# A hybrid decoder layer on one core: the indexer key centred and doubled by one product, rotary partners by VectorE shuffles, index scores in fours

## What is computed

```python
q_idx = partial_rope(q_idx.reshape(B, T, IDX_HEADS, IDX_DIM), positions)   # 8 heads x 64
k_idx = layernorm(k_idx, k_norm_w, k_norm_b)                               # one key of 64
k_idx = partial_rope(k_idx[:, :, None, :], positions)[:, :, 0, :]
w_idx = w_idx * (IDX_HEADS ** -0.5 * IDX_DIM ** -0.5)
...
s = jnp.einsum('bqhd,bsd->bqhs', qi, k_idx)
score = jnp.einsum('bqh,bqhs->bqs', wi, jax.nn.relu(s))
score = jnp.where(key_pos <= tq, score, -inf)
```

## Time and profile before

| | us |
|---|---|
| median of 3 executions | 726.9 (726.54 to 729.52) |
| the profiled execution, its own time | 728.42 |
| its span on the core | 726.7 |
| mean granted TensorE clock | 0.991 |
| PE busy | 705.7 |
| DVE busy | 434.0 |
| ACT busy | 296.2 |

### The profile page before, as it was taken

One profiled execution on the slowest core, in us unless ns is written; L12 is line 12 of the kernel. 1 busy time (PEld: TensorE's weight loads), 2 busy tenths in 40 slices (PEclk: granted clock), 3 DMA queues, 4 the chain that ended last, 5 costly groups with the idle time before them and its releaser, 6 DMA issues.

```text
span 726.7 us, 11020 instructions
## 1 busy us (share of the span) xinstructions
PE 705.7 (97%) x3962; PEld 552.7 (76%) x3962; DVE 434.0 (60%) x806; ACT 296.2 (41%) x472; POOL 11.1 (2%) x39
## 2 busy tenths in 40 slices
PE   5999999999999999999999999999999999999997
PEld 4565567777766878878888888888888788888885
DVE  3966678898898999968643433323432335443444
ACT  6445553535454444536572343342343332211223
POOL 4000000000000000000000000000000000000000
PEclk9999999999999999999899999999999999999999
DMA  9944023231222766567225532355533224223202
GB/s 314 358 144 114 3 59 85 62 116 53 62 60 87 217 217 223 182 209 205 81 59 145 144 105 78 106 144 144 144 94 108 87 87 132 99 87 102 71 0 117
DMA packets 95995, 89.10 MB, mean 123 GB/s; under 512 B 2950, under 2 KB 84954, under 8 KB 95964
## 3 DMA queue, kind: packets, MB, share of 16 engines
q1 hardware_dynamic: 95964, 88.70, 39.9%
HBM read 86.59 MB, written 2.10 MB: 122 GB/s over the span
## 4 chain that ended last, share of the span: by engine, by line
PE 61%; DVE 4%; issue 1%; ACT 0%; DVEq 0%; ACTq 0%
PE ps L1342 34%; PE ps L1363 17%; PE ps L1381 6%; DVE rope L892 1%; PE ps L1646 1%; PE ps L1402 1%; PE ps L1529 1%; DVE w_lo L817 1%; PE ps L1666 1%; PE ps L1778 1%; PE ps L1782 1%; PE ps L1779 1%; PE ps L1523 0%; DVE act L1149 0%; DVE res L1154 0%
## 5 line engine op out<-in xcount | busy, mean ns | idle before, releaser
L1342 PE MATMUL ps<-h_hi,w_hi 128*128 128x512 f32 x560 | 227.3, 406 | 0.0
L1342 PE MATMUL ps<-h_hi,w_lo 128*128 128x512 f32 x560 | 218.7, 391 | 0.0
L1342 PE MATMUL ps<-h_lo,w_hi 128*128 128x512 f32 x560 | 218.3, 390 | 0.0
L817 DVE TENSOR_TENSOR w_lo<-w_raw,w_hi 128x1024 fp32r<-128x1024 f32 (+1 forms) x109 | 129.3, 1187 | 99.4 <-ACT w_hi L462 98.9
L462 ACT ACTIVATE w_hi<-w_raw 128x1024 fp32r<-128x1024 f32 (+1 forms) x109 | 111.6, 1029 | 105.9 <-PE ps L1363 86.3
L1342 PEld LDWEIGHTS ps<-h_hi,w_hi 128*128 128x128 f32 x560 | 105.2, 188 | 30.3 <-issue 9.1
L1342 PEld LDWEIGHTS ps<-h_hi,w_lo 128*128 128x128 f32 x560 | 105.1, 188 | 22.6
L1342 PEld LDWEIGHTS ps<-h_lo,w_hi 128*128 128x128 f32 x560 | 105.3, 188 | 20.7 <-issue 1.0
L1363 PE MATMUL ps<-w_hi,h_hi 128*128 128x512 f32 x176 | 70.1, 398 | 0.8 <-DVE mix L1214 0.8
L1363 PE MATMUL ps<-w_hi,h_lo 128*128 128x512 f32 x176 | 68.6, 390 | 0.0
L1363 PE MATMUL ps<-w_lo,h_hi 128*128 128x512 f32 x176 | 68.5, 389 | 0.0
(11 more groups left out here) (250 smaller groups left out, 791.9 us busy)
## 6 DMA issues: line engine op xcount, KB each, us to landing
w_raw<-in_w_ffn_in SPq DMA_DIRECT2D x44, 512.0 KB, 5.7
w_raw<-in_w_in SPq DMA_DIRECT2D x28, 512.0 KB, 3.8
w_raw<-in_w_ffn_out SPq DMA_DIRECT2D x22, 512.0 KB, 3.5
adaw<-in_w_ada SPq DMA_DIRECT2D x12, 512.0 KB, 3.9
act<-in_w_ada SPq DMA_DIRECT2D x12, 512.0 KB, 9.2
adaw<-in_w_ada SPq DMA_DIRECT2D x6, 1024.0 KB, 5.3
act<-in_w_ada SPq DMA_DIRECT2D x6, 1024.0 KB, 5.1
res<-in_x SPq DMA_DIRECT2D x8, 512.0 KB, 4.7
```

The costliest lines, as they stand in the source:

```text
L817: V.tensor_tensor(w_lo[slot][:, 0:n], w_raw[slot][:, 0:n], w_hi[slot][:, 0:n].bitcast(f32), ALU.subtract).then_inc(lo_ok, 1)
L1342: last = mm(ps[bank][0:rows, :], a, b, start=(k == 0 and n == 0), stop=(k == KT - 1 and n == 2))
```

## The change

1. The key. `dup` becomes the doubling matrix minus 1/64 in its 64 rows, so that one product on 64 rows, written to all 128, centres and doubles the key. The product for the mean, the key's partner product and the separate doubling go, and so do DVE's centring and ACT's copy of `ik`. Square, variance product, logarithm, exponential, scaling and rotation of the key now run on 128 rows. The norm's weight and bias are loaded to both halves of the rows, so SP issues four small DMAs in place of two.
2. The partner rows. DVE's `stream_shuffle` makes them, one for the key and one for each of the four query tiles; the four `idx_partner` products and `swap_idx` go, with three instructions of POOL (one comes for `dup`).
3. The scores. `SCORE_ORDER` takes heads 0 to 3 of tiles 1, 2, 3 first, then heads 4 to 7. PE makes four products, then two projection steps, six times. Query tile 3 is rotated between the first and the second four of DVE's sums. Eleven projection steps stand ahead of the scores, unbroken, and nine behind.
4. On ACT the split of weight slot 2 moves from ahead of the key's square to behind its exponential.

```diff
+PARTNER_IDX = [(r + 8) % 16 if r < 16 else r for r in range(32)]
+SCORE_ORDER = [(t, h + 4 * half) for half in range(2) for t in range(1, SEQ // P) for h in range(4)]
@@ sync
-            sp.dma_start(knorm[0:IDX_DIM, 0:1], ...)
-            sp.dma_start(knorm[0:IDX_DIM, 1:2], ...)
+            for at in (0, IDX_DIM):
+                sp.dma_start(knorm[at:at + IDX_DIM, 0:1], ...)
+                sp.dma_start(knorm[at:at + IDX_DIM, 1:2], ...)
@@ gpsimd
-            step(pool.memset(swap_idx[:, :], 0.0))
-            for lo in range(2):
-                ...
+            step(pool.tensor_scalar(dup[0:IDX_DIM, :], dup[0:IDX_DIM, :], 1.0 / IDX_DIM, None, ALU.subtract))
@@ scalar
+            copy_idx(0)
+            copy_idx(1)
+            copy_idx(2)
+            sc.wait_ge(ikc_mm, 1)
+            sc.activation(relu[0], ps[7][:, :], ACT.Square).then_inc(iksq_ok, 1)
+            copy_idx(3)
+            copy_idx(4)
...
+            sc.activation(relu[1], ps[6][:, :], ACT.Ln, scale=1.0 / IDX_DIM, bias=eps[:, :]).then_inc(ikln, 1)
+            sc.wait_ge(ikln, 1)
+            sc.activation(relu[1], relu[1], ACT.Exp, scale=-0.5).then_inc(ikr_ok, 1)
+            split_hi(2, U_HG[2], G_HG - 1)
             split_hi(3, U_HG[3], G_HG)
-            sc.wait_ge(ikd_mm, 1)
-            sc.activation(ik, ps[7][:, :], ACT.Copy).then_inc(ik_ok, 1)
@@ vector
-            def rotate(dst, partner, cos, sin, n, t1, t2):
-                V.tensor_tensor(t1, dst, cos, ALU.mult)
-                V.tensor_tensor(t2, partner, sin, ALU.mult).then_inc(idx_t, 1)
+            def rotate(dst, src, n, t1, t2):
+                V.stream_shuffle(t2, src, PARTNER_IDX).then_inc(idx_swap, 1)
+                V.tensor_tensor(t1, src, cos_i, ALU.mult)
+                ve.wait_ge(idx_swap, n + 1)
+                V.tensor_tensor(t2, t2, sin_i, ALU.mult).then_inc(idx_t, 1)
                 ve.wait_ge(idx_t, n + 1)
                 V.tensor_tensor(dst, t1, t2, ALU.add).then_inc(idx_ok, 1)
...
+            rotate_iq(0, 0)
+            ve.wait_ge(ikr_ok, 1)
+            V.tensor_tensor(r_tmp, ps[7][:, :], relu[1], ALU.mult).then_inc(ikn_step, 1)
+            ve.wait_ge(ikn_step, 1)
+            V.tensor_scalar(r_tmp, r_tmp, knorm[:, 0:1], knorm[:, 1:2], ALU.mult, ALU.add).then_inc(ikn_ok, 1)
+            ve.wait_ge(ikn_ok, 1)
+            rotate(ik, r_tmp, 1, relu[0], r_tmp2)
+            rotate_iq(1, 2)
+            split_lo(G_HG + 2, 2)
+            rotate_iq(2, 3)
+            ve.wait_ge(wt_ok, 1)
+            score_four(0)
+            rotate_iq(3, 4)
+            score_four(4)
+            split_lo(G_HG + 3, 3)
+            for n in range(8, 24, 4):
+                score_four(n)
@@ tensor
+            mm(ps[7][:, :], dup[0:IDX_DIM, :], ikw[0:IDX_DIM, :], start=True, stop=True).then_inc(ikc_mm, 1)
...
+            mm(ps[6][:, :], ones[0:IDX_DIM, :], relu[0][0:IDX_DIM, :], start=True, stop=True).then_inc(ikv_mm, 1)
+            hg_project(0, 0, 11)
...
-            for n in range(0, 24, 2):
-                score_mm(n)
-                score_mm(n + 1)
-                hg_project(0, 12 + n // 2, 13 + n // 2)
-            hg_project(0, 24, 32)
+            for n in range(0, 24, 4):
+                for m in range(n, n + 4):
+                    score_mm(m)
+                hg_project(0, 11 + n // 2, 13 + n // 2)
+            hg_project(0, 23, 32)
```

More of the change, by code:

```diff
@@ L105, in build @@
         dup = sb("dup", P)
-        swap_idx = sb("swap_idx", P)
         prm_rows = sb("prm_rows", P)
@@ L194, in build @@
         idx_swap, idx_t, idx_ok = sem("idx_swap"), sem("idx_t"), sem("idx_ok")
[L195 to L198, removed]
+        ikc_mm, iksq_ok, ikv_mm, ikln, ikr_ok = (sem(n) for n in (
+            "ikc_mm", "iksq_ok", "ikv_mm", "ikln", "ikr_ok"))
+        ikn_step, ikn_ok, wt_mm, wt_ok = (sem(n) for n in ("ikn_step", "ikn_ok", "wt_mm", "wt_ok"))
         sc_mm, sc_relu, sc_acc, causal_ok = sem("sc_mm"), sem("sc_relu"), sem("sc_acc"), sem("causal_ok")
@@ L259, in _ @@
             sp.dma_start(rc[:, :], rope_const).then_inc(pos_loaded, 16)
[L260 to L261 removed]
+            for at in (0, IDX_DIM):
+                sp.dma_start(knorm[at:at + IDX_DIM, 0:1], idx_k_norm_w.rearrange("o p -> p o")).then_inc(pos_loaded, 16)
+                sp.dma_start(knorm[at:at + IDX_DIM, 1:2], idx_k_norm_b.rearrange("o p -> p o")).then_inc(pos_loaded, 16)
             load_idx(1)
@@ L553, in _, with copy_idx @@
             split_hi(1, U_HG[1], G_HG - 2)
-            for at, n in enumerate(IDX_ORDER):
+            def copy_idx(at):
+                n = IDX_ORDER[at]
                 rows = IK_COLS if n == 4 else P
@@ L672, in score_relu @@
             def score_relu(n):
-                t = n // IDX_HEADS + 1
+                t = SCORE_ORDER[n][0]
                 sc.wait_ge(sc_mm, n + 1)
@@ L979, in _ @@
                 if pair == 0:
-                    ve.wait_ge(pos_loaded, 64)
+                    ve.wait_ge(pos_loaded, 96)
                     astep(V.tensor_copy(pos, pos_i[:, :].bitcast(i32)))
@@ L1001, in rotate_iq, with score_four @@
             def rotate_iq(n, at):
-                ve.wait_ge(idx_swap, at + 1)
+                ve.wait_ge(idx_raw, n + 2)
                 if at:
                     ve.wait_ge(idx_ok, at)
[L1005 to L1032, removed]
+                rotate(iq[:, n * SEQ:(n + 1) * SEQ], iq[:, n * SEQ:(n + 1) * SEQ], at, o_n, o_rstd)
+            def score_four(first):
+                for n in range(first, first + 4):
+                    t, h = SCORE_ORDER[n]
                     ve.wait_ge(sc_relu, n + 1)
@@ L1038, in _ @@
                     else:
-                        ve.wait_ge(sc_acc, n)
+                        ve.wait_ge(sc_acc, n if h != 4 else n - 8)
                         V.scalar_tensor_tensor(out=sc_t[t], in0=r, scalar=w, in1=sc_t[t], op0=ALU.mult,
                                                op1=ALU.add).then_inc(sc_acc, 1)
[L1042 to L1048, removed]
+                if first >= 12:
+                    ve.wait_ge(sc_acc, first + 4)
+                    V.tensor_tensor(sc_t[t][:, t * P:(t + 1) * P], sc_t[t][:, t * P:(t + 1) * P], bias_t[0],
+                                    ALU.add).then_inc(causal_ok, 1)
+            rotate_iq(0, 0)
[15 more added lines that the diff above has]
+                score_four(n)
             ve.wait_ge(causal_ok, TT - 1)
@@ L1488, in _ @@
             idx_low(KT - 1)
[L1490 to L1495, removed]
             def hg_project(hh, start, end):
@@ L1539, in _ @@
             last.then_inc(wt_mm, 1)
-            mm(ps[7][kd, :], ones[kd, kd], ikw[kd, :], start=True, stop=True).then_inc(ikm_mm, 1)
-            idx_partner(0, 0)
-            idx_partner(1, 1)
             te.wait_ge(iksq_ok, 1)
[L1544 to L1555, removed]
+            mm(ps[6][:, :], ones[0:IDX_DIM, :], relu[0][0:IDX_DIM, :], start=True, stop=True).then_inc(ikv_mm, 1)
+            hg_project(0, 0, 11)
             te.wait_ge(wt_ok, 1)
+            te.wait_ge(idx_raw, 5)
             def score_mm(n):
-                t, h = n // IDX_HEADS + 1, n % IDX_HEADS
+                t, h = SCORE_ORDER[n]
                 rows = slice(IDX_DIM * (h % 2), IDX_DIM * (h % 2) + IDX_DIM)
```

12 lines of the change are left out of this document (2 added, 10 removed).

## The result

The change takes 722.34 us, median of 4 executions (721.61 to 723.57), against 728.15 of the kernel before in the same session (4, 726.54 to 729.52): ratio 0.9926, 95% interval 0.9909 to 0.9944, which is 5.8 us less (4.1 to 6.6). On another chip it was 722.32 (6 executions) against 727.48 (11): 0.9932, 0.9915 to 0.9949, 5.2 us less. The forecast was 722.0, 4.9 us less than the 726.9 that it started from.

The account below looks back on a forecast made before the run. PE bound the index stage; of its 7.9 us saving DVE's queue allowed 5.7, and PE's waits for Relus put level 0 at 99.0 instead of 103.91: 726.9 - 4.9 = 722.0 us, range 719.0 to 725.2.

Parts of the forecast that it names:

- What leaves PE: PE's index stage: the mean, four query partner products, the key's partner and an idle bracket go, together 6.1 us.
- The fours on PE: PE's score products: six of twelve switches go, 1.2 us, and second pairs start behind running products, 0.6 us.
- DVE's queue: DVE from the key's exponential (64.3) to level 0's factor (98.2), without slack: level 0 at most 5.7 us sooner.
- The shuffle: DVE's rotations: a shuffle on 128 rows was taken to cost 0.72 us, as on 32 rows.
- rival of 32-row groups in turn: DVE's shuffles: groups of 32 rows go in turn, 2.9 us each, level 0 at 108.5, time 731.5; chance 0.06.
- Where PE waits: PE ahead of products 12 to 19, 80 to 88 us: about 3 us of waits, level 0 at 99.0.
- Edits at no cost: Start: two more small DMAs delay later loads by up to 1.2 us, under cover; POOL gets two small instructions less.
- The fours lock the engines: Rival, products 8 to 19: hand-overs lose 0.15 us more each, 1.8 us in all, time 723.8; chance 0.15.
- All of PE's saving arrives: Rival, index stage: DVE is 2.2 us or more faster than its rows, full 7.9 saved, 719.0; chance 0.1.
- The clock in the gaps: Rival, PE's gaps in the index stage: the granted clock falls, costing 1.7 us, time 723.7; chance 0.06.

Follow-up runs that it names:

- pairs: The change with two products and one projection step twelve times instead of fours, new head order kept: 721.09 us against 727.33 before, ratio 0.9910, stage 38.53.
- both orders undone: The change with scores in the old order, two products and one step, all rotations ahead of the sums: 725.16 us against 727.62 before, ratio 0.9964.
- shorter rotations: The change with the four query tiles rotated for tokens 128 to 511 only: 723.54 us, one execution, stage 38.50.
- later split: The change with only DVE's split of weight slot 3 moved from behind sum 7 to behind sum 15: 722.1 us, one execution, stage 38.54.
- both edits again: Repeat of the change with queries rotated for tokens 128 to 511 only and slot 3 split after sum 15: 721.7 us against 727.48 before, ratio 0.9918.
- pairs with both edits: The change with tokens 128 to 511 rotated, slot 3 split after sum 15, two products per step: 720.4 us against 727.48 before, ratio 0.9916.

## Why the prediction was right

The mechanism came true: DVE's queue caps the gain, and PE's saving beyond it turns into holds. That the time of 722.0 was met within 0.4 us is partly luck. It starts from 726.9, the median of three executions; with a fourth the kernel before has 728.15, and the gain was 5.8 and 5.2 us on two chips, 5.33 in the stage, where 4.9 was forecast. By its own steps:

- **What leaves PE**, 6.1: from the stage's start to the first score there were 17.78 us with twelve steps, and are 10.82 with eleven. With a step at 0.68 that is 6.3.
- **The fours on PE**, 1.8: undersized. They save 2.4 to 2.5 (37.8 with pairs), so PE's own work is 35.4 (predicted 36.2).
- **DVE's queue**, 33.9 from exponential to factor: 33.36. The exponential comes 4.6 after the stage's start (4.5), scaling and affine take 1.3 (1.3), the steps behind the sums 2.6 (2.6). The rotations are the term that is too large: the key's takes 2.75 to the next instruction, the three others 2.54 to 2.57, together 10.4 (10.9). The experiments with doubled shuffles and with pairs show that this queue sets the end.
- **The shuffle** at 0.72, the row on 32 rows: 0.72 to 0.75 on 128 rows, 0.733 on average over the four of the queries, so that the rival of 32-row groups in turn is out. The estimate of 0.6 us from the Trainium skill, VectorE: DVE Perf Modes, section "The perf-mode tier table", is low by about a fifth; the table has its time in the column for bf16, and these values are float32.
- **Where PE waits**: about 3 us ahead of products 12 to 19, put down to Relus. Measured 3.4, 3.0 of it before and in the fourth and fifth group; only 0.47 shows as an idle bracket, where brackets for the whole were forecast. The path held: Relu 15 was to end 27.2 after the stage's start and ended after 26.7, and from there to the level product it is 12.1 (12.0). The level product was to come 39.2 after the stage's start, and came after 38.8: gain 5.3 for 4.9. The 0.4 is the shorter queue of DVE; the fours' larger saving on PE went into larger holds. DVE is 0.84 ahead (0.8).
- **Edits at no cost**: the DMAs held, by the experiment that delays the two added ones. The unchanged kernel's start moved by 0.9 between its two profiles, so the later start (+1.5) is put down to scatter; no run settles all of it.
- **The fours lock the engines**: half right as a mechanism. The locks take all that the fours save on PE (2.5), but the forecast already had them in its 3 us; they took 0.4 more, and not the rival's 1.8.
- **All of PE's saving arrives**: out, since the stage is 38.8 and not 36.2. It is the kernel with both orders undone that tells why the order is needed at all: PE would wait for rotations.
- **The clock in the gaps**: not in the change, whose granted clock is 1.00 in 86 to 89 us, right behind the holds; PE was busy for 2.95 of the 3.00 us before. With shuffles doubled it fell there, behind a bracket of 1.04 us. Windows of that kernel:

```profile
83.00:86.00 3.00, 1.91 (x6) 0.88 (x6) 2.69 (x6) 2.18 (x5) 0.00 (x0) 1.00 0.00 0
86.00:89.00 3.00, 2.97 (x9) 1.88 (x8) 2.72 (x4) 1.14 (x3) 0.00 (x0) 0.72 0.26 47
89.00:92.00 3.00, 3.00 (x11) 1.35 (x11) 2.62 (x6) 1.62 (x5) 0.00 (x0) 0.71 0.44 133
```

By the rule of the Trainium skill, TensorE: Matmul & The Clock Gate, section "A second HAM failure mode: psum-queue depth-cycling", the change's short holds could have brought such falls. Its trace does not agree; the trace with longer holds does, once, at a cost within 0.5 us, since DVE's queue set the end there (expected 41.9, measured 42.4).

## What to carry to other kernels

When work leaves the busiest engine, sum the queue of the next one between the two events that bound the stage: here 33.9 us of VectorE rows gave the new length to 0.4 us, where the 7.9 us taken from TensorE did not. The length of that queue is not enough: where the order of heads was undone, the same instructions on VectorE gave a stage 1.9 us longer, since TensorE wanted the last rotations first. Grouping products on TensorE, no longer the bound, only moved time into waits here; ordering the consumers so that late producers are wanted late is what paid. Judge an edit of about 1 us by the stage in the trace and by many executions, and look at the granted clock in the stage first, since one fall of it is worth as much as the edit.

## What was not expected of the hardware

**A fall of the granted clock with PE busy.** Five of the twelve profiles of the change and its variants (doubled shuffles, shorter rotations, later split, both edits again, pairs with both edits) have 0.80 to 0.94 in 61 to 65 us and 0.64 to 0.77 in 65 to 69; neither of the two profiles of before has. PE was busy for 4.00 of 4.00 us, with plain float32 products and then projection steps. From the stage's start to the first score it costs about 1.5 (12.35 to 12.39 for 10.82). The change's own profiles do not show it; whether the change makes it likelier stays open.

**A second place, near 350 us,** far behind the change. Windows of the kernel before, of the change and of the one with doubled shuffles:

```profile
350.00:360.00 10.00, 9.71 (x58) 9.47 (x57) 6.22 (x11) 4.38 (x11) 0.00 (x0) 0.66 0.18 54
```

```profile
350.00:360.00 10.00, 9.41 (x50) 8.21 (x49) 7.91 (x16) 6.72 (x13) 0.00 (x0) 0.87 0.19 54
```

```profile
350.00:360.00 10.00, 9.41 (x67) 8.44 (x67) 9.57 (x17) 7.75 (x15) 0.00 (x0) 1.00 0.19 54
```

From 340 to 350 us the change has 0.96, the other two 1.00. What the clock lacks of 1.00 in the 20 us from 340 to 360 adds up to 3.4, 1.7 and 0 us, and from the level product to the span's end it is 622.8, 621.2 and 619.7 us. So the profile of before carries 1.6 us more of this than the change's, which hides the change's later start. In its second profile the kernel before has 0.83 in the window and 621.1 us, as the change: there the spans differ by 4.6 us, 5.3 of stage less 0.6 of start and 0.1 of the rest.
